# A hybrid diffusion layer on one core: the first weight tiles one modulation unit later, and the first norm split around unit 2's products

## The reference, cut to what matters

```python
ml = (silu(c) @ w_ada + b_ada).reshape(B, N_MOD, D)        # latent stream
mc = (silu(c_ctx)[None] @ w_ada + b_ada).reshape(1, N_MOD, D)   # context stream
h = x + pos_embed_2d(rows, GRID_W, D)
u  = modulate(rmsnorm(h, norm_g[0]),  ml[:, 0], ml[:, 1])   # u * (1 + scale) + shift
uc = modulate(rmsnorm(hc, norm_g[0]), mc[:, 0], mc[:, 1])
gate, up = split(u @ ffn_w_in[0])                            # 2048 -> 2 x 5632
h = h + 0.5 * ml[:, 2] * ((silu(gate) * up) @ ffn_w_out[0])
```

## Time and profile before

| | |
|---|---|
| median of three runs | 2898.59 us |
| profiled execution, its own time | 2895.85 us |
| its span | 2894.0 us |
| PE busy | 2829.6 us (98%) |
| DVE, ACT, POOL busy | 1646.8, 967.8, 214.0 us |
| mean granted clock of PE | 0.987 |

### The profile page before, as it was taken

How to read it: one execution, slowest core, us unless ns; L and a number is a source line. 1 busy time by engine, 2 the same in 40 slices (tenths; PEclk the granted TensorE clock), 3 DMA queues, 4 the chain that set the end, 5 groups by cost and what they waited for, 6 DMA issues and landing times. The chain is left out here.

```text
span 2894.0 us, 47636 instructions
## 1 busy us (share of the span) xinstructions
PE 2829.6 (98%) x17840; PEld 2483.3 (86%) x17840; DVE 1646.8 (57%) x2212; ACT 967.8 (33%) x1443; POOL 214.0 (7%) x373
## 2 busy tenths in 40 slices
PE   6899999999999999999999999999999999999998
PEld 3688888888888888888888888878999999999998
DVE  4456676776776752223225766755675555555555
ACT  2222222222222222111213555544354444444444
POOL 0000000000000000000101013545120000000001
PEclk8899999999999999999999999999999999999999
DMA  8766666667888865554553566685556555565554
GB/s 335 285 207 195 223 218 200 221 200 245 310 297 317 292 227 192 192 193 163 193 195 110 155 194 190 189 268 176 161 174 188 190 188 187 184 188 189 188 189 145
DMA packets 410320, 604.41 MB, mean 209 GB/s; under 512 B 52960, under 2 KB 303840, under 8 KB 401520
## 3 DMA queue, kind: packets, MB, share of 16 engines
q1 hardware_dynamic: 361824, 419.52, 45.5%
q10 hardware_dynamic: 48400, 183.63, 18.5%
HBM read 560.02 MB, written 43.02 MB: 208 GB/s over the span
## 5 line engine op out<-in xcount | busy, mean ns | idle before, releaser
L1945 DVE TENSOR_TENSOR wl<-raw,wh 128x1024 fp32r<-128x1024 f32 x638 | 781.6, 1232 | 823.4 <-ACT wh L1470 821.0
L1470 ACT CAST wh<-raw 128x1024 fp32r<-128x1024 f32 x638 | 664.4, 1047 | 1452.4 <-PE ps L763 1429.5
L762 PE MATMUL ps<-xl,wh 128*128 128x512 f32 (+1 forms) x2560 | 972.9, 380 | 0.0
L761 PE MATMUL ps<-xh,wh 128*128 128x512 f32 (+1 forms) x1904 | 727.0, 382 | 15.5 <-DVE wl L1945 15.5
L763 PE MATMUL ps<-xh,wl 128*128 128x512 f32 (+1 forms) x1904 | 720.0, 378 | 0.0
L762 PEld LDWEIGHTS ps<-xl,wh 128*128 128x128 f32 x2560 | 484.7, 189 | 90.6
L761 PEld LDWEIGHTS ps<-xh,wh 128*128 128x128 f32 x1904 | 360.8, 190 | 91.3 <-issue 21.4
L763 PEld LDWEIGHTS ps<-xh,wl 128*128 128x128 f32 x1904 | 361.2, 190 | 67.5
L761 PE MATMUL ps<-x2h,wh 128*128 128x256 f32 x1408 | 394.1, 280 | 1.7 <-DVE x2l L2015 1.7
L762 PE MATMUL ps<-x2l,wh 128*128 128x256 f32 x1408 | 395.3, 281 | 0.0
L763 PE MATMUL ps<-x2h,wl 128*128 128x256 f32 x1408 | 393.8, 280 | 0.0
(11 more groups left out here) (276 smaller groups left out, 2650.5 us busy)
## 6 DMA issues: line engine op xcount, KB each, us to landing
raw<-in_ffn_w_in SPq DMA_DIRECT2D x704, 256.0 KB, 3.4
raw<-in_ffn_w_out SPq DMA_DIRECT2D x176, 512.0 KB, 3.8
abuf<-in_w_ada ACTq DMA_DIRECT2D x64, 1024.0 KB, 6.8
abuf<-in_w_ada ACTq DMA_DIRECT2D x96, 512.0 KB, 3.9
xl<-d_h ACTq DMA_DIRECT2D x80, 512.0 KB, 3.3
ada_t<-in_ada SPq DMA_DIRECT2D x64, 512.0 KB, 8.0
raw<-in_w_in SPq DMA_DIRECT2D x128, 256.0 KB, 3.4
raw<-in_w_out SPq DMA_DIRECT2D x32, 512.0 KB, 5.0
```

Source lines behind the costliest of these rows:

```text
L761: mm(out, ah, bh, start=first, stop=False, skip_group_check=reopened)
L762: mm(out, ah, bl, start=False, stop=False, skip_group_check=reopened)
L1470: nc.scalar.copy(wh[:, t % HL, :], raw[:, t % RAW, :]).then_inc(hi_done, 1)
L1945: tt(tl, raw[:, t % RAW, :], th.bitcast(F32), ALU.subtract).then_inc(lo_done, 1)
```

## The change

The table of tiles moves each tile one unit later and loses its last entry, which the old code excluded with a condition; `norm` is cut in two functions, and in the first stage the sums stand ahead of unit 2's products and the broadcast behind them, ahead of unit 1's columns. The last norms of the kernel call the two halves in one piece as before.

```diff
-FIRST_TILES = {2 * t + 3: t for t in range(K_TILES - 1)}
+FIRST_TILES = {2 * t + 4: t for t in range(K_TILES - 2)}
...
             def norm(n, nt, bank):
-
+                norm_sums(n, nt, bank)
+                norm_rms(n, nt, bank)
+
+            def norm_sums(n, nt, bank):
 
                 pe.wait_ge(nacc_done, sums_at(n, KT - 3))
                 pe.wait_ge(sq_done, squares_at(n, KT - 2))
...
                 i.then_inc(stat_pe, 1)
+
+            def norm_rms(n, nt, bank):
+
                 pe.wait_ge(rstd_done, rms_at(n))
...
             def first_groups():
                 pe.wait_ge(cpad_set, 2)
                 for i in range(ADA_SS):
+                    if i == 2:
+                        norm_sums(0, NTOK, 7)
                     if i >= 2:
                         pe.wait_ge(arow_set, i - 1)
                     for q in range(ADA_Q):
...
+                    if i == 2:
+                        norm_rms(0, NTOK, 7)
                     if i:
                         ada_columns(i - 1, 6)
-                    if i == 2:
-                        norm(0, NTOK, 7)
                     k = FIRST_TILES.get(i)
-                    if k is not None and i < ADA_SS - 1:
+                    if k is not None:
                         pe.wait_ge(x_ready, 2 * k + 2)
                         up_tile(0, 0, k, 0, k)
```

## The result

The changed kernel takes 2883.18 us (median of 4 runs, 2882.56 to 2884.17), the kernel before 2899.5 us (4 runs, 2892.53 to 2902.66). The ratio is 0.9947, with a 95% interval of 0.9929 to 0.9966: faster by about 16 us, where 24 (from the profiled execution) were forecast. The direction was right; the likeliest time, 2873 us, came out 10 us too low, and 2883.18 lies above the forecast's own range of 2866 to 2879.

A forecast was written before the change was run, and what follows sets the result against it. PE bounds the kernel; the change acts in the first 160 us. Block 12 earlier by 22.9, plus 1.6, minus 0.5, gives 24.0 us: 2871.9 from the profile, 2874.6 from the median, predicted 2873, range 2863 to 2884 (forecast's own 2866 to 2879).

The forecast's parts named there:

- The waits: First 160 us: PE's waits for DVE's split before weight tiles (L761), 7 times, 14.8 us, would go.
- The transfers as the next bound: Modulation stage: at 401 GB/s a pair of units and a tile need 11.8 us, more than PE's 10.56.
- The refill gap: Behind tile 0: unit 7 waits for unit 5's slot, data flow from 56.4; block 12 at 112.7, otherwise 110.1.
- The head: Norm and first units: earlier norm lets tile 0 start at 46.0 instead of 47.08, held by DVE.
- The base: Whole kernel: 24.0 us off the profiled 2895.85 gives 2871.9, the stage's gain reaching the end whole.
- the closing blocks: After the tiles: block 12 takes 1.6 us less at full clock; 0.5 taken off for a wait at block 15.
- The clock: Tiles 1 to 5: without waits they run at full clock, 9.95 us less than their old 38.75.
- The clock falls again: Rival, tiles: waits for transfers replace those for DVE and tiles still start at half clock; 2879 us, chance 0.13.
- The transfers run at their old mean: Rival, modulation stage: transfers stay at 334 GB/s because of size or order; 2881 us, chance 0.07.
- The columns' wait: Rival, units: PE waits at the columns instead of the tile, cold tiles stay; 2890.5 us, chance 0.06.
- the clock at 1.2 GHz over the stage: Rival, slower: the norm's sums lower the clock and interleaved units never raise it; 2929 us, chance 0.04.

The follow-up runs named there:

- the second one after: The changed kernel run and profiled once more without an edit: 2880.29 us (10 runs), ratio 0.9953 to the kernel before.
- The third profile after: The changed kernel profiled a further time without an edit: 2872.07 us in its one execution.

## Why the prediction was right, and where it failed

*The waits: right.* They went from L761, at all five tiles and at block 12; the wait did not move to the columns.

*The transfers as the next bound: right.* 400 GB/s, a period of 11.7 to 11.9 us (11.8 forecast), waits for ada_t in small pieces. Halving the bytes brought it to 10.39, near the 10.56 worked out for PE alone. The Trainium skill's 358 GB/s per core ("DMA: Bandwidth & Descriptors", section "Where 436 GB/s comes from") is not the bound of this kernel, which runs on one core alone: this trace has 400 over 47 us.

*The refill gap: right number, in part by luck.* Block 12 was forecast at 112.7 with the gap and 110.1 without. The gap came in the first profile (block 12 at 114.84), where a cold tile 0 held the ring's slots longer; without it block 12 stands at 112.07 and 112.04, and a longer ring moves nothing. Both cases lie some 2 us above their forecast. Without the gap it is the start: the prediction let the data of units 5 and 6 flow from 42, but PE waits for the last quarter of unit 4 until 44.45 and for that of unit 6 until 56.10, against 53.8. With the gap 0.8 of it is tile 0's later end (54.59 against 53.8), and the rest was not followed up.

*The head: right number, wrong reason.* Tile 0 was forecast at 46.0 because DVE would still be at split 0. It came at 45.49 to 46.36, and what PE waits for ahead of it is unit 4's data behind a full queue, until 44.40 to 44.48 in all four profiles, as in the second one after:

```profile
44.45 0.64 PE L769 MATMUL ps<-ada_t,cpad 128*32 128x256 f32 x8 [0.64 <-DMA ada_t<-in_ada]
```

With half the bytes tile 0 starts at 43.34, behind DVE. So the earlier norm is hidden behind the transfers, and whether its new order gives the 1.1 us reckoned for it is not shown: with the norm in one piece tile 0 came at 45.42, but in an execution whose norm was 2.8 us early.

*The base: the step by which the time failed.* The sum takes 24.0 us from "the profiled execution's own 2895.85" and lets the gain "reach the end whole, since PE's work behind it stays the same". The work stayed the same, but not its time. In the profile of the base the rest behind block 12 was 2760.2 us, with the step of 113.4 ns, which ten of the thirteen profiled executions did not have. Less the 1.6 and plus the 0.5 us of the closing blocks the forecast has 2759.1 us behind block 12; the first profile after has 2768.4. These 9.3 us and the 2.1 us by which block 12 is late are the whole distance from 2871.9 to 2883.20. With block 12 as forecast and the other end, 2769 (mean of the five in the table), the sum is 2882. The third profile after shows the other side of it: block 12 at 112.04 and the same end as the base give 2872.07 us, and 2871.9 was the sum. That the base's total lies only 2.7 us below the median hid this: it had a dear stage and a cheap end.

*The clock: the step by which the gain failed.* The term of 9.95 us for tiles 1 to 5, with 1.6 at block 12, has the right mechanism: filling the waits alone brings all tiles to 5.62 to 5.66 us. Its size was read from one execution in which every tile behind a wait was cold. In two of four profiles of the same kernel two tiles of five and block 12 run at full clock behind the same 2.2 us, and the tiles cost 32.6 us, 6.1 less. Block 12 stands at 130.8 us in the mean of the four profiles before and at 113.6 after: the stage gains 17.2 us where 22.9 were forecast. Of the 4.8 us by which the profile of the base lies above that mean, 3.1 are tiles 1 to 5, 1.2 tile 0 and 0.6 its start. Block 12 itself, to the next columns, takes 4.45, 2.88, 4.45 and 2.90 us before and 2.83 to 2.84 after: 0.8 less in the mean, where 1.6 were forecast. The 0.5 us taken off for a wait at block 15 is not seen: no profile after has such a wait up to 150 us.

*The rivals.* "The clock falls again" happened to single tiles, not to all: tile 0 cold in two of four profiles after (8.31 and 7.51 us), tile 2 in one; block 12 comes some 3 us later in these two. The Trainium skill's warning ("TensorE: Matmul & The Clock Gate", section "HAM oscillation") is of a wait longer than the tile's compute, behind which each tile starts cold. No wait here is that long: 19 of 20 tiles 1 to 5 after run at full clock (5.63 to 5.68 us) among waits of up to 0.9 us, while before 18 of 24 pieces were cold behind 2.2 us, also less than a tile takes. "The transfers run at their old mean" named 2881, close to the result, by a mechanism that the trace refutes: 400, not 334 GB/s. The columns' wait and the clock at 1.2 GHz over the stage are not seen. The reason given for the latter was misread: unit 2 ran at half clock ahead of the norm's sums, not beside them (from 27.54, the sums from 33.17).

*Like with like:* profiles with 117.8 ns have 2898.7 before (two) and 2882.8 after (three), 15.9 us apart; those with 113.4 ns 2891.6 (two) and 2872.07 (one), 19.5.

## What to carry to other kernels

A gain that is read from one profiled execution carries that execution's luck: where a term rests on the granted clock behind waits, take the price with all tiles cold and with none as the bounds, and choose inside them. That a profile's total lies near the median does not make its stages typical, so a stage's change is better added to a median rest than to that profile's own. And when a wait goes, the next bound can be forecast from the bytes and the rate of a full queue.

## What the runs showed of the hardware that was not expected

A wait of 2.1 to 2.2 us ahead of a tile or block brought the half clock in 18 of the 24 cases of tiles 1 to 5 and block 12 in the four profiles of before; one of 0.4 us, with the rest filled by small matmuls, in none of 6. What decides among equal waits of one execution stays open.

The same 2112 matmuls of 256 columns, with the same program and no idle time between, start every 113.4 ns in three profiled executions and every 117.8 in ten, which is worth 9.3 us of 2880; the up matmuls of the same shape between them take 117.8 in both cases. Both kernels show both values, and they do not go with the clock of the first stage (both are found with five cold tiles, with three and with none). The granted clock is 1.00 in both cases (2192 to 2210 us, first two profiles of before). Its cause was not found, and no experiment was made on it.
